# Modulation rows as weighted sums on VectorE and GpSimd instead of matrix products on TensorE

## What is computed

```python
mod = jnp.einsum('bd,de->be', jax.nn.silu(c), w_ada[l]) + b_ada[l]      # block 1: 1 vector x (1024, 3072)
shift, scale, gate = jnp.split(mod, 3, axis=-1)
h = rms_norm(x, norm_pre[l]) * (1.0 + scale[:, None, :]) + shift[:, None, :]
...
x = x + gate[:, None, :] * rms_norm(mix, norm_post[l])
# block 2: two vectors (latent and context) x (1024, 6144)
mod = (s_lat @ w_ada[l] + b_ada[l]).reshape(B, N_MOD, 1, D)
mod_c = (s_ctx @ w_ada[l] + b_ada[l]).reshape(N_MOD, 1, 1, D)
p_l = modulate(x, norm1_g[l], mod[:, 0], mod[:, 1]) @ w_in[l]
p_c = modulate(ctx, norm1_g[l], mod_c[0], mod_c[1]) @ w_in[l]
...
```

## Time and profile before

| | us |
|---|---|
| median of 3 runs | 1870.52 |
| the three runs | 1866.34 to 1871.33 |
| span of the profiled execution | 1876.8 |
| start and first four chunks | 0 to 37 |
| first projection | 37 to 223 |
| first attention, with chunks 4 to 15 | 223 to 316 |
| output projection, chunks 16 and 17 | 316 to 391 |
| the rest of block 2 | 391 to 1877 |

### The profile page before, as it was taken

How to read it: one execution, slowest core, us unless ns; L and a number is a source line. 1 busy time by engine, 2 the same in 40 slices (tenths; PEclk the granted TensorE clock), 3 DMA queues, 4 the chain that set the end, 5 groups by cost and what they waited for, 6 DMA issues and landing times.

```text
span 1876.8 us, 37887 instructions
## 1 busy us (share of the span) xinstructions
PE 1717.6 (92%) x16822; PEld 927.4 (49%) x16822; DVE 804.7 (43%) x1484; ACT 518.8 (28%) x983; POOL 109.4 (6%) x144
## 2 busy tenths in 40 slices
PE   5999999999999999999999999999999977778786
PEld 3444566544546555556667667544454333323332
DVE  3853144656627456355654554344462211222210
ACT  3710254311127422354453341122231110101010
POOL 0000010010000000100000000000001101010100
PEclk8999989999989999999998998899999999999998
DMA  9121376351110030042221210356569999999997
GB/s 396 76 88 47 145 287 247 145 224 69 45 45 1 23 151 0 17 170 82 77 81 50 63 56 24 114 219 221 219 239 398 416 425 415 422 413 425 417 423 279
DMA packets 48360, 359.25 MB, mean 191 GB/s; under 512 B 8325, under 2 KB 8557, under 8 KB 28736
## 3 DMA queue, kind: packets, MB, share of 16 engines
q1 hardware_dynamic: 35792, 311.51, 41.2%
q0 software_dynamic: 12400, 45.27, 7.3%
HBM read 337.47 MB, written 27.32 MB: 194 GB/s over the span
## 4 chain that ended last, share of the span: by engine, by line
PE 74%; DMA 16%; ACT 4%; issue 3%; DVE 2%; POOL 0%; SPq 0%; ACTq 0%; DVEq 0%; POOLq 0%
PE psum L207 71%; DMA arena<-in_w 16%; PE psum L210 3%; ACT arena L204 3%; ACT L204 1%; DVE arena L154 1%; DVE arena L180 0%; DVE arena L164 0%; DVE arena L172 0%; DVE arena L160 0%; POOL arena L141 0%; DMA arena<-in_tok 0%; DVE arena L168 0%; DVE arena L159 0%; POOL out L149 0%
## 5 line engine op out<-in xcount | busy, mean ns | idle before, releaser
L207 PE MATMUL psum<-arena 32*32 32x16 f32 (+12 forms) x16178 | 1638.1, 304 | 145.2 <-DMA arena<-in_w 73.4
L207 PEld LDWEIGHTS psum<-arena 32*32 32x32 f32 (+5 forms) x16178 | 856.0, 135 | 876.3 <-issue 764.7
L204 ACT ACTIVATE arena<-psum 128x512 f32<-128x512 f32 (+5 forms) x334 | 171.4, 513 | 871.2 <-PE psum L207 670.7
L154 DVE TENSOR_TENSOR arena<-arena,psum 128x512 f32<-128x512 f32 (+3 forms) x128 | 64.9, 507 | 402.6 <-PE psum L207 209.2
L154 DVE TENSOR_TENSOR arena<-arena 128x512 f32<-128x512 f32 (+10 forms) x315 | 191.6, 608 | 31.0 <-ACT arena L204 14.7
L204 ACT ACTIVATE arena<-arena 128x512 f32<-128x512 f32 (+10 forms) x254 | 138.8, 546 | 177.7 <-DVE arena L154 41.9
L204 ACT ACTIVATE arena<-psum,arena 128x128 f32<-128x128 f32 (+3 forms) x221 | 111.7, 505 | 275.1 <-PE psum L210 135.5
L154 DVE TENSOR_TENSOR arena<-psum,arena 128x128 f32<-128x128 f32 (+3 forms) x116 | 47.4, 409 | 154.5 <-PE psum L207 141.3
L164 DVE SCALAR_TENSOR_TENSOR arena<-arena 128x512 f32<-128x512 f32 (+7 forms) x162 | 103.5, 639 | 14.5 <-ACT arena L204 8.1
L210 PE MATMUL psum<-arena 128*128 128x128 f32 x644 | 102.6, 291 | 6.1 <-ACT arena L204 3.2
L172 DVE RECIPROCAL arena<-arena 128x1 f32<-128x1 f32 (+4 forms) x71 | 79.1, 1113 | 63.0 <-ACT arena L204 59.2
(11 more groups left out here) (49 smaller groups left out, 177.7 us busy)
## 6 DMA issues: line engine op xcount, KB each, us to landing
arena<-in_w SPq DMA_DIRECT2D x127, 2048.0 KB, 34.5
arena<-in_w SPq DMA_DIRECT2D x48, 256.0 KB, 3.1
arena<-in_w SPq DMA_DIRECT2D x12, 1024.0 KB, 36.4
arena<-kd POOLq DMA_DIRECT2D x28, 256.0 KB, 3.4
gd<-arena SPq DMA_DIRECT2D x24, 256.0 KB, 3.2
arena<-gd SPq DMA_DIRECT2D x24, 256.0 KB, 5.6
arena<-in_w POOLq DMA_DIRECT2D x2, 2048.0 KB, 9.6
kd<-arena POOLq DMA_DIRECT2D x2, 1536.0 KB, 11.0
```

What stands on the lines that cost most here:

```text
L154: return self.ends(self.e.tensor_tensor(out, a, b, op))
L204: return self.ends(self.e.activation(out, a, func, **kw))
L207: return self.ends(self.e.matmul(out, lhs, rhs, start=start, stop=stop))
```

## The change

PE no longer multiplies chunks 4 to 17. Each chunk is loaded in four parts of 512 KB, two row blocks each, by GpSimd's queue into two 1024-column buffers. For each vector v that the chunk serves (one for j = 4, 5 and 10 to 17, two for j = 6 to 9), the row blocks are scaled by `cs[:, k, v]`, one number for each partition, and added up in one of four sums of 128x512. Parts 0 to 23 (chunks 4 to 9) are summed by DVE, two instructions for each part and vector, in the slots `ADA_PARTS` of the first projection (tiles 9 to 11 and 13 to 22). Parts 24 to 55 (chunks 10 to 17) are summed by GpSimd with a multiply in place and an add for each row block. PE then only adds the 128 partitions of a sum: four products for each sum, with a column of ones at column v of the stationary block, at the places `ADA_SUMS`. DVE copies the result, and an accumulating transfer adds it to the bias, which is copied to `mods1` and `mods2` beforehand. SP's ring has no modulation chunk from 4 on any more.

```diff
-MAIN_CHUNKS = [0, 1, 2, 3, 6, 7, 8, 9, 10, 11, 4, 5, *range(14, 24), 12, 13, 24, 25, *range(26, 34), *range(40, 45)]
+MAIN_CHUNKS = [0, 1, 2, 3, 6, 7, 8, 9, 10, 11, 12, 13, *range(26, 34), *range(40, 45)]
...
+        ADA = range(4, 18)
+        ADA_VECTORS = {j: (0,) if j < 6 else (1, 2) if j < 10 else (1,) for j in ADA}
+        ADA_SUMS = {("p1", 12): 4, ("p1", 13): 5, ("p1", 18): 6, ("p1", 20): 7, ("p1", 22): 8, ("att", 2): 9, ("att", 18): 10, ("att", 28): 11,
+                    ("out1", 1): 12, ("out1", 2): 13, ("pool", 1): 14, ("pool", 3): 15, ("q", 1): 16, ("k", 0): 17}
...
+        def ada_part_gpsimd(n):
+            j, q = 4 + n // 4, n % 4
+            s, v = ada_at(j, 1) % 4, ADA_VECTORS[j][0]
+            G.wait_ge(d_aw[n % 2][n])
+            if q == 0:
+                G.wait_ge(T["ada", ADA_SLOTS[ada_at(j, v) - 4][0]])
+            for k in range(2):
+                w, by = ada_in[n % 2][:, k, :], cs[:, 2 * q + k, v:v + 1]
+                if q == 0 and k == 0:
+                    G.ts(ada_sum[s], w, by, None, ALU.mult)
+                else:
+                    G.ts(w, w, by, None, ALU.mult)
+                    G.tt(ada_sum[s], ada_sum[s], w, ALU.add)
+            G.then_inc("part", n)
...
+        def ada_load(n):
+            if n > 1:
+                G.wait_ge(ada_by(n - 2)["part", n - 2])
+            G.dma(ada_in[n % 2].rearrange("p k n -> p (k n)"), T_["w"][ada_chunk(j), :, 1024 * q:1024 * q + 1024], d_aw[n % 2].up(n))
...
+        def ada_part_vector(n):
...
+                    if q == 0 and k == 0:
+                        V.ts(ada_sum[s % 4], w, by, None, ALU.mult)
+                    else:
+                        V.stt(ada_sum[s % 4], w, by, ada_sum[s % 4], ALU.mult, ALU.add)
...
+        def ada_tensor(j, ring):
+            T.wait_ge(ada_by(4 * j - 13)["part", 4 * j - 13], *ps.take(ring, "ada", j))
...
+                    T.mm(ps["ada", j][32 * t:32 * t + 32, 0:128], one_column(v), ada_sum[ada_at(j, v) % 4][:, c4(t)],
...
         def lru_gpsimd():
             G.dma(nbb, T_["norm_att"].partition_broadcast(128), d_na.up("na"))
-            G.dma(bias, T_["bias"], d_bias.up("bias"))
-            for j in range(4, 16):
-                if j == 10:
+            G.dma(mods1, T_["bias1"], d_bias.up("mods1"))
+            G.dma(mods2, T_["bias2"], d_bias.up("mods2"))
+            STORES = {10: 4, 11: 5, 18: 6, 22: 7, 24: 8, 31: 9, 37: 10, 45: 11, 49: 12, 53: 13}
+            for n in range(56):
+                ada_load(n)
+                if n > 24:
+                    ada_part_gpsimd(n - 1)
+                if n in STORES:
+                    ada_gpsimd(STORES[n])
+                if n == 31:
                     G.wait_ge(V["yan"], *mods_stored(5))
...
+            ada_part_gpsimd(55)
```

More of the change, by code:

```diff
@@ L729, in pre_vector @@
             V.zero(cs)
+            V.zero(cs[:, 0, 16:17], value=1.0)
             V.wait_ge(A["cs_sg"], d_par["par"])
@@ L1031, in att_tensor @@
                     T.then_inc("pv1", x - 3)
-            for step in steps:
-                ada_tensor(*step, MBANK)
         def att_gated_tensor(i):
@@ L1363, in proj2_vector @@
                     late.step()
-                    continue
-                late.add(pooled(m) if n == "pool" else normed(n, m))
+                else:
+                    late.add(pooled(m) if n == "pool" else normed(n, m))
+                if before[n, m] in ADA_SUMS:
+                    ada_vector(ADA_SUMS[before[n, m]])
+                for part in ADA_PARTS.get((n, m), ()):
+                    ada_part_vector(part)
                 if (n, m) == ("pool", 3):
```

101 lines of the change are left out of this document (58 added, 43 removed).

## The result

The kernel after takes 1953.23 us (median of 4 runs, 1949.17 to 1958.12), the kernel before 1870.92 beside it (4 runs): a ratio of 1.044, 95% interval 1.041 to 1.047. It is slower, as forecast, but by 82 us instead of 13, and outside the range. The profiled run of after is 1949.17 us, its span 1947.4, which is 70.6 above the span of before (1876.8); the 12 us to the 82 arise since the profile of after is the shortest of its runs and that of before lies 6 us above its median. Of e9 one execution and of e10 two fell in a slower state of the chip, and medians and ratios leave these three out.

A forecast was written before the change was run, and what follows sets the result against it. PE was taken to set the pace in the three changed stages; terms of +6.0, -17.0, -4.6 and +1.0 gave -14.6 us, but the wait for `in_ropes` at 411 made it +13.3: 1870.5 to 1884 us, range 1854 to 1922.

The forecast's parts named there:

- The GpSimd chain: GpSimd's 32 parts from 229 us, 5.3 us on average, ahead of issuing `in_ropes` and `in_pool_w`; end at 403.6.
- R - 397.7: Shift of the program at pool tile 0 when R is late; +13.3 us at 411, hidden below R = 383.
- R: Time at which `in_ropes` lands, behind GpSimd's parts, needed by DVE for pool tile 0; put at 411 us.
- the upper end: GpSimd's arithmetic priced as three streams and a second pass for the scalar: 1.8 us for each instruction.
- rival 4: GpSimd much slower, 6.5 us a part, `in_ropes` at 449: +51 us, 1922; chance 0.10.
- the serial value: GpSimd's reads and writes pass one after the other: multiply 0.95 us, add 1.37 us, from memset rows.
- Attention, -17.0 forecast: First attention: -21.1 us of modulation products leaving PE, +3.2 of new idle time, +0.9 of sums.
- The step's price: Attention: four modulation products cost 0.22 us, so a step loses 0.66; block 1 falls to about 1.5 us.
- the forecast's sum without the wait: First projection, attention, output projection and second projection together, if nobody waits for GpSimd: -14.6 us.
- First projection, +6.0 forecast: First projection: +1.9 us of PE products, +2.4 at tile 12, DVE starting the attention 1.7 late (0 to 8).
- Output projection, -4.6 forecast: Output projection: PE's wait for chunk 26 and chunks 16 and 17 go, -5.1 us; two sums add 0.5.
- rival 3: DVE and GpSimd block each other, R growing by up to 37 us: +30 us, 1900; chance 0.12.

The follow-up runs named there:

- e9: Kernel before with only chunks 16 and 17 summed by GpSimd, early in the first projection; 1879.07 us against 1870.95, ratio 1.0044.
- e10: Kernel before with chunks 14 to 17 summed by GpSimd during the first projection; 1876.65 us against 1868.89, ratio 1.0037.
- e8: e1 with each of GpSimd's multiplies by one number per partition written as a product of two tensors; 1911.45 us (one run).
- e11: e1 with VectorE's parts 16 to 23 cut to one column, twelve idle products in the attention's first eight steps, chunk 9's sum at step 9; 1901.08 us.
- e1: Kernel after with the four tables of the second projection issued by SyncE's queue instead of behind GpSimd's parts; 1902.97 us, ratio 1.014 to before.
- e14: Kernel before, all products kept, with three 128x512 adds on VectorE ahead of the first attention; 1898.27 us (2 runs), ratio 1.016.
- e5: Kernel before, all products kept, with six 128x512 adds on VectorE ahead of the first attention; 1932.38 us (one run; before 1870.95).
- e13: e1 with GpSimd's multiplies and adds cut from 512 to 32 columns, same number of instructions, loads and stores; 1896.6 us, ratio 1.014 to before.
- e2: Kernel before with chunks 4 to 17 multiplied only by their last row block, nothing added on VectorE or GpSimd; 1889.68 us (one run).
- e12: e1 with VectorE's parts 16 to 23 cut to one column, four idle products in each free attention step, chunk 9's sum moved; 1913.95 us (one run).

## Why the prediction was wrong, step by step

- **The GpSimd chain: right mechanism, mis-sized term; this put the time outside the range.** The shift of R - 397.7 holds: VectorE took up the pool tile at R = 470.8, which gives +73.1 for 70.6 measured. R was put at 411, and these 60 us cover the whole miss (70.6 for 13.3), since in this formula nothing else counts once R is late. Three terms made them. The multiply: 0.95 forecast from the memset row, 1.75 measured, near the upper end of 1.8 (64 x 0.8 = 51 us). It is slower than the add (1.29 for 1.37 forecast, 56 x -0.08 = -4.5), which no model by streams gives; e8 shows that it is the form with one number for each partition that is slow. The start: 235.4 instead of 229, 6.4 us, since the store of chunk 8 ahead of it waited 4.25 us for VectorE's copy. The rest, some 7 us of 60, is in hand-overs, in issues of stores at 0.93 us instead of 0.55, and waits for loads. A part took 7.0 us on average (228 us for 32, with some 5 us of stores in them) where 5.3 was forecast and rival 4 had 6.5. The choice of the serial value over the upper end was the mistake: the memset row has no scalar operand and bounds a multiply only from below. In the Trainium skill (GPSIMD Engine Reference, Performance versus the Vector engine) the add is 1.17 us, as an estimate from its 4497 ns, and 1.26 was measured at least: that holds to 0.1 us. The Trainium skill (GPSIMD Engine Reference, Engine selection) also has operations with one input at about line rate, an estimate of 0.55 us for the multiply. For it 1.56 us at best was measured, so that does not hold here.
- **Attention, -17.0 forecast, +9.6 measured: the step whose mechanism failed.** The prediction took for granted that TensorE stays at the clock of the earlier trace rows, 0.94, when a third of its instructions remain and idle times appear, and gave this neither a price nor a chance. It went to 1.2 GHz and stayed there for 95 us. The step's price was not the fault: at the full clock a step takes 1.16 us in e11 where the forecast's 2.16 - 0.66 is 1.50. The trace of before held the sign of it: behind its 1.11 us of idle time the clock was low for 10 us. The prediction itself said that a stage not shorter by 15 us would refute its reading of the products; what fell was not their price but the clock at which the rest would run.
- **The two failures don't add up in after.** Had the attention given its 17 us, VectorE would only have waited longer for R: in after the lost gain costs nothing. It shows as soon as the wait is gone, in e1, which is still 28 us over before, where the forecast's sum without the wait was -14.6.
- **First projection, +6.0 forecast, +10.0 measured.** The stall at tile 12 is 3.03 us for 2.4. VectorE's parts ended at 232.0 instead of 226, because each waited for its load (14.8 us in all), and TensorE waited 3.68 and 0.79 us at the attention's start, first for VectorE and then for ACT, where 1.7 was forecast. Inside the bound of 8. What wasn't seen is that such an idle time also costs the clock: e14 and e5 price one of 2.1 us at this place at 24 to 34 us and one of 4.3 at 54 to 61, with all else as before.
- **Output projection, -4.6 forecast, +1.7 measured.** The wait for chunk 26 did go; in its place stand 0.99, 2.09 and 5.39 us for VectorE. The forecast was right but for rival 3: the stage alone gave 4.9 us in e9, and in e13, with GpSimd's arithmetic cut, it takes 73.1 us, 4.1 less than the 77.2 of before (391.39 less VectorE's last combination at 313.34 and the 0.83 that lie behind it in after). In the Trainium skill (SBUF — State Buffer, Who interferes with whom) it is a rule that a VectorE instruction with both inputs in SBUF and a GpSimd instruction that reads SBUF exclude each other; e13 against e1 agrees, with 1225 and 1959 ns. It works both ways: GpSimd's multiply took 2.00 us in this stage and 1.65 in the attention, where VectorE has few such instructions. So rival 3 has a part in R too: the mean of 1.75 lies 0.19 over the best of 1.56, 12 us for 64 multiplies.
- **The rivals.** Rival 4 (6.5 us a part, 1922) was nearest on the part, rival 3 happened with it, and none had the clock in it. The range ended at rival 4; by the same formula the measured R would have given 1944, and a rival of a slow multiply and the blocking together was not there. The direction came out as forecast and for the forecast's reason, R; e1 shows that it would have come out slower without it too, for a reason that the forecast did not have.

**Settled and open.** Settled by runs: 42 us go with the place of `in_ropes` behind the chain (e1), 6 to 7 us of the output projection with GpSimd's work beside VectorE (e13), and removing most of the products from the whole attention makes it 14 us longer even where nothing is added (e2, one run), while removing them from its last five steps gives 4.2 us (e10). An idle time of 2 us at the attention's start, with all products in place, lost the clock for 50 us (e14). Open is what decides whether the clock falls and how soon it comes back: with all products and 1.1 us it took 10 us or did not fall at all (e9), with 2.1 us 50, with 4.3 us over 120, each in one trace; with thinned products it came back only in the last steps of the stage; and in e12 it fell with no idle time near. Idle time and thin steps both matter, and no run here parts them cleanly. No run had more than some 7 us of thin steps at the full clock in one piece, so what the change would be worth there, the 76 us of the prediction, stays an estimate. No version was faster than before.

## What to carry to other kernels

Work taken from TensorE between short dependent steps is not a gain by its duration: look first at the granted clock behind the idle times that are already in the trace, in more than one execution, and give the case in which the stage runs at 1.2 GHz a price and a chance. Ahead of a chain of some hundred microseconds on GpSimd, move every transfer that someone else waits for to another queue, and price GpSimd's arithmetic from a run of the very form, since a factor of 1.8 in one form of instruction, used 64 times, became 50 us. And where a slack engine is given work, what counts is whether it is on time at the next stage's start.

## What the runs showed of the hardware that was not expected

- GpSimd scales 128x512 by one number for each partition in 1.56 us at best and 1.75 on average, and adds two tensors of that size in 1.26 and 1.29; the multiply written as a product of two tensors takes 1.29.
- TensorE at full occupancy in the records can stay at 0.50 of its clock for over 120 us (e5, windows from 233 to 353), behind one idle time of 4.28 us. Behind the same idle time of 1.1 us it was low for 10 us in two traces and not at all in a third (before, e10; e9).
- VectorE's add of 128x1024 with both inputs in SBUF goes from 1225 to 1734 ns (1959 in e1) beside GpSimd's arithmetic, and GpSimd's multiply from 1.65 to 2.00 us where it stands beside more of them.
